# State-space stage of a two-block network: squares in eight tiles, two G and two V tables under the input product, lag zero on TensorE, states a quarter ahead

## The chip, the cores and the metric

The kernel runs on one core of one Trainium2 chip. The metric is the device time of the launch in microseconds. A measurement is the median of several runs of the same program.

## The reference

The reference computes two blocks one after the other on a sequence of 512 tokens of width 1024, in float32. The change touches only the first layer of the first block, the state-space mixer:

```python
u = (rms_norm(x) @ w_in).reshape(seq, 64 groups, 16)
a = exp(lam * step)                      # complex, 64 states per group
bu = einsum('gnk,lgk->lgn', b * f, u)    # complex
x_l = a * x_(l-1) + bu_l                 # scan over the 512 tokens
y = real(einsum('gkn,lgn->lgk', c, x)) + d_skip * u
z = gelu(y);  val, gate = split(z @ w_glu);  x = x + val * sigmoid(gate)
```

Behind it come a feed-forward layer, a latent attention layer, a second feed-forward layer and the whole second block (three kinds of attention in two layers).

## The kernel before

The kernel is written in raw instructions: every engine has a program of its own in the order in which it is to run, and semaphores join them. Nothing is planned by a compiler, so an instruction that waits holds all that stands behind it on its engine.

Matrix products use split operands. A weight block of 128 output channels (1024 inputs) is loaded by SP into one of four `raw` slots (`load`), ScalarE writes its high half `wh` (L583, `split_high`), VectorE the low half `wl` (L1088, `split_low`), each with two slots, and `product` (L1819) runs 24 matmuls of 512 columns: high by high, high by low, low by high (L1828 to L1830). `ahead` splits the block two places ahead.

The input product (stage `w_in`, blocks 0 to 7) takes `xH` and `xL`, which ScalarE (L597) and VectorE (L1094) make tile by tile. In product 0 each of the eight input tiles is followed by a matmul of ones by its square (L1967); the squares go through two buffers, so ScalarE (L600) waits on TensorE (`sq_used`). `inverse_root` (L607) turns their sum into the row `R`. Between the tiles VectorE computes the factors of the recurrence (`denominator`, `input_gain`, `powers`, `gained`, all through L1128), then `input_sums` and `output_sums`. Each finished block is multiplied by `R` into `T` (L1274) and written by SP to DRAM (L434), from where `read_u` (L418) reads it back with channels and time rearranged, eight transfers per quarter into `U`. Quarter 1 lies over `T[0:2]`, so its read waits for all eight blocks.

The recurrence is done in chunks of eight steps, in four quarters of 16 groups. For a quarter q:

- `make_g(q)` (VectorE, L1213 on, five instructions of 128x1024) makes the table G, of which there is one; `from_g` (TensorE, L1867) transposes it into `WM` through ScalarE copies (L641, `copy_w`), `lags` (L1878) multiplies it by `C2` (ScalarE, L650) into the lag weights, and `lag0` (VectorE, L1283 on) adds the skip term to them and writes them as the last row of `MS`. SP copies that row seven times, shifted (`mat_shift`, L429).
- `make_v(q)` (POOL, L484 to L488, five instructions of 128x1024) makes the table V. There is one, so for q above 0 it waits for `y_ready` of the quarter before.
- `states(q)` (TensorE, L1893) makes the chunks' inputs; VectorE rotates them by the phases `Er`, `Ei` (six instructions), scans (L1326, two) and rotates back into `state` (six).
- `outputs(q)`: the Toeplitz part (L1906: `MS` by `U`), then the state part (L1914: V by `state`), which sets `y_ready`. ScalarE applies gelu (L691), `turn_z` (L1924) transposes, ScalarE and VectorE split the result into `zH` (L677) and `zL` (L1303).

POOL makes the phase tables before V: five rounds of doubling, then the last third alone (L526 to L528); VectorE makes the other part in `last_phases` (L1232), after block 6. TensorE's order is: products 0 to 6, `from_g(0)`, `lags(0)`, product 7, and then for each quarter `states(q)`, `from_g(q+1)`, `turn_z(q-1)`, `lags(q+1)`, `outputs(q)`; in the last quarter half of the first two glu blocks (L1938 to L1940) goes in front of `outputs`. VectorE's order in a quarter is: rotation, `zL` of the quarter before, scans, state, `make_g(q+2)`, `lag0(q+1)`; `make_g(1)` and `lag0(0)` stand between product 7 and the first rotation. SP's order behind the input product is, for each quarter, the seven shifts of `MS`, the wait for `y_ready`, and the eight reads of the quarter two ahead.

## Time and profile before

| what | value |
|---|---|
| median of 3 runs | 1985.24 us (1982.36 to 1986.06) |
| profiled execution | 1985.31 us, span 1983.5 us |
| granted TensorE clock over the span | 0.977 |
| TensorE busy | 1860.6 us (94%), 8948 matmuls |
| VectorE busy | 1068.1 us (54%) |
| ScalarE busy | 833.3 us (42%) |
| GpSimd (POOL) busy | 131.8 us (7%) |
| HBM traffic | 143.83 MB read, 4.19 MB written |

In the profile PE is TensorE's matmuls and PEld its weight loads, DVE is VectorE, ACT ScalarE, POOL GpSimd, SP the engine that issues most transfers; the letter q behind an engine is its sequencer. A group names line, engine, operation, output and inputs. "Idle before" is the time for which the engine stood still just before, and the name behind the arrow is what ended it. PEclk is the granted clock as a share of 2.4 GHz. Times are from the span's start.

### The profile page before, as it was taken

What the parts mean: (1) busy time and instruction counts of PE and PEld (TensorE: products, weight loads), DVE (VectorE), ACT (ScalarE), POOL (GpSimd) and SP (SyncE); (2) the same over time, 40 slices, a digit from 0 to 9 for tenths busy, and PEclk for the clock granted to TensorE, in tenths of its full rate; (3) what the DMA queues carried; (4) which work ended last, traced back from release to release, by engine and by line L of the source; (5) the groups of instructions that cost most, each with busy time, mean ns of one, the idle gap of its engine ahead of it and who ended that gap; (6) DMA issues with size and microseconds to landing.
All of it is one profiled execution on the core that took longest, in us unless ns stands there. A gap on an engine that the chain in (4) does not pass through costs nothing.

```text
span 1983.5 us, 24248 instructions
## 1 busy us (share of the span) xinstructions
PE 1860.6 (94%) x8948; PEld 1429.4 (72%) x8948; DVE 1068.1 (54%) x1640; ACT 833.3 (42%) x1393; POOL 131.8 (7%) x164
## 2 busy tenths in 40 slices
PE   6787999999999889989999999999999989999997
PEld 4676878888888656657888888778666667866665
DVE  7695454444433657746444434464555375456537
ACT  4231344444223556744444422232566532266653
POOL 7543000000000000000000000001000000100000
PEclk9888999999999999999999999999999999999998
DMA  4320322222333110112222233312111022311111
GB/s 171 98 51 32 104 88 95 95 96 100 92 97 102 45 33 26 60 41 92 99 95 95 95 93 93 101 68 92 54 54 54 33 85 75 96 54 43 54 34 63
DMA packets 56827, 151.18 MB, mean 76 GB/s; under 512 B 15744, under 2 KB 20640, under 8 KB 56736
## 3 DMA queue, kind: packets, MB, share of 16 engines
q1 hardware_dynamic: 55232, 148.31, 22.7%
q0 software_dynamic: 1504, 1.64, 0.3%
q8 instruction: 59, 0.97, 0.2%
q14 instruction: 32, 0.26, 0.0%
HBM read 143.83 MB, written 4.19 MB: 75 GB/s over the span
## 4 chain that ended last, share of the span: by engine, by line
PE 84%; DVE 10%; ACT 4%; issue 2%; DMA 0%; POOL 0%; DVEq 0%; SPq 0%; ACTq 0%
PE bank L1828 17%; PE bank L1829 17%; PE bank L1830 17%; PE bank L2312 3%; PE bank L2314 3%; PE bank L2313 3%; PE bank L2289 2%; PE bank L2274 1%; PE bank L2275 1%; PE bank L2273 1%; PE bank L2033 1%; DVE wl L1088 1%; DVE G L1128 1%; PE bank L2061 1%; ACT wh L583 1%
## 5 line engine op out<-in xcount | busy, mean ns | idle before, releaser
L1088 DVE TENSOR_TENSOR wl<-raw,wh 128x1024 fp32r<-128x1024 f32 (+3 forms) x280 | 324.5, 1159 | 545.8 <-ACT wh L583 543.2
L583 ACT ACTIVATE wh<-raw 128x1024 fp32r<-128x1024 f32 (+3 forms) x280 | 279.0, 997 | 617.6 <-PE bank L1830 520.6
L1828 PE MATMUL bank<-xH,wh 128*128 128x512 f32 x896 | 358.6, 400 | 11.4 <-DVE wl L1088 9.5
L1829 PE MATMUL bank<-xL,wh 128*128 128x512 f32 x896 | 350.7, 391 | 0.0
L1830 PE MATMUL bank<-xH,wl 128*128 128x512 f32 x896 | 350.5, 391 | 0.0
L1828 PEld LDWEIGHTS bank<-xH,wh 128*128 128x128 f32 x896 | 169.6, 189 | 53.6 <-issue 15.7
L1829 PEld LDWEIGHTS bank<-xL,wh 128*128 128x128 f32 x896 | 169.5, 189 | 38.9 <-issue 4.1
L1830 PEld LDWEIGHTS bank<-xH,wl 128*128 128x128 f32 x896 | 169.3, 189 | 35.8
L1828 PE MATMUL bank<-hidH,wh 128*128 128x512 f32 x352 | 137.3, 390 | 0.0
L1830 PE MATMUL bank<-hidH,wl 128*128 128x512 f32 x352 | 136.9, 389 | 0.0
L1829 PE MATMUL bank<-hidL,wh 128*128 128x512 f32 x352 | 136.9, 389 | 0.0
L2312 PE MATMUL bank<-xH,wh 128*128 128x512 f32 x256 | 109.8, 429 | 10.7 <-ACT qk L961 7.1
L2314 PE MATMUL bank<-xH,wl 128*128 128x512 f32 x256 | 101.5, 396 | 0.0
L2313 PE MATMUL bank<-xL,wh 128*128 128x512 f32 x256 | 100.9, 394 | 0.0
L1728 DVE TENSOR_REDUCE least<-bank 128x1 f32<-128x128 f32 (+3 forms) x96 | 42.5, 485 | 73.8 <-PE bank L2296 73.8
L952 ACT ACTIVATE Pm<-bank,least 128x128 f32<-128x128 f32 (+3 forms) x96 | 49.9, 525 | 68.5 <-DVE least L1728 68.4
L1829 PEld LDWEIGHTS bank<-hidL,wh 128*128 128x128 f32 x352 | 66.1, 188 | 14.0 <-issue 0.2
L1828 PEld LDWEIGHTS bank<-hidH,wh 128*128 128x128 f32 x352 | 66.1, 188 | 13.9 <-issue 0.2
L1830 PEld LDWEIGHTS bank<-hidH,wl 128*128 128x128 f32 x352 | 66.1, 188 | 13.8
L2312 PEld LDWEIGHTS bank<-xH,wh 128*128 128x128 f32 x256 | 48.7, 190 | 22.0 <-issue 15.7
L720 ACT ACTIVATE hidH<-T 128x512 f32 (+1 forms) x44 | 27.8, 632 | 78.6 <-DVEq L1374 78.6
L552 POOL DMA_DIRECT2D rope_cos<-con_dram x2 | 1.1, 556 | 884.7 <-PE bank L2218 884.7
(424 smaller groups left out, 3311.7 us busy)
## 6 DMA issues: line engine op xcount, KB each, us to landing
raw<-w_gu_dram SPq DMA_DIRECT2D x88, 512.0 KB, 3.4
raw<-w_p_dram SPq DMA_DIRECT2D x64, 512.0 KB, 3.4
raw<-w_dn_dram SPq DMA_DIRECT2D x32, 448.0 KB, 3.3
raw<-w_glu_dram SPq DMA_DIRECT2D x16, 512.0 KB, 3.6
raw<-w_dn_dram SPq DMA_DIRECT2D x16, 512.0 KB, 3.5
raw<-w_out_dram SPq DMA_DIRECT2D x16, 512.0 KB, 3.5
raw<-w_in_dram SPq DMA_DIRECT2D x8, 512.0 KB, 7.8
raw<-w_o_dram SPq DMA_DIRECT2D x8, 512.0 KB, 3.4
```

The costliest lines, as they stand in the source:

```text
L583: nc.scalar.activation(wh[:, (st.base + u) % 2, 0:kts * P], raw[:, (st.base + u) % 4, 0:kts * P], ACT.Copy).then_inc(w_high, 1)
L720: nc.scalar.activation(hidH[:, bass.ds(2 * i + u // 2, 1), :].rearrange("p o n -> p (o n)"), T[:, 3, :], ACT.Copy).then_inc(sem("hid_high" ...
L952: nc.scalar.activation(Pm[side][:, POFF[j]:POFF[j] + w], banks[side][:, 0:w], ACT.Exp, scale=-1.0, bias=least[:, j, side:side + 1], accum_ ...
L1088: nc.vector.tensor_tensor(wl[:, s, 0:kts * P], raw[:, (st.base + u) % 4, 0:kts * P], wh[:, s, 0:kts * P].bitcast(F32), ALU.subtract).then_ ...
L1728: nc.vector.tensor_reduce(least[:, j, side:side + 1], banks[side][:, 0:(j + 1) * P], AX, ALU.min)\
L1828: nc.tensor.matmul(bank, wh[:, s, w], hi[:, k, :], start=first and kt == 0, stop=False)
L1829: nc.tensor.matmul(bank, wh[:, s, w], lo[:, k, :], start=False, stop=False)
L1830: ins = nc.tensor.matmul(bank, wl[:, s, w], hi[:, k, :], start=False, stop=last and kt == kts - 1)
L2289: nc.tensor.matmul(banks[side][:, 0:w], qk[half_of(side), m, j * P:w], qk[half_of(side), 8 + m, 0:w], start=True, stop=False)
L2312: nc.tensor.matmul(bank, wh[:, s, w], xH[:, kt, :], start=kt == 0, stop=False)
L2313: nc.tensor.matmul(bank, wh[:, s, w], xL[:, kt, :], start=False, stop=False)
L2314: ins = nc.tensor.matmul(bank, wl[:, s, w], xH[:, kt, :], start=False, stop=kt == KD - 1)
```

## The change

The state-space stage is put in another order, with more buffers:

- the eight squares get a tile each (four in `T`, two in `sq`, `acc`, `sd`), and their matmuls stand in one block behind product 1; the ones come from the constants, which SP loads earlier, and the loads of blocks 1 to 3 change places with `Bz` and `Cz`;
- the input blocks use other banks (`in_bank`), so that banks 1, 2 and 0 come free for `states(0)` and `lags(1)`;
- `make_g(0)` is cut in two parts, between evictions; its transposes and lag weights stand behind product 4; `make_g(1)` stands behind the eviction of block 4, `states(0)` and the first half of `from_g(1)` before product 7;
- V has buffers of its own for quarters 1 and 3; `make_v(0)` goes in front of POOL's last phases, `make_v(1)` behind the eviction of block 7;
- lag zero: POOL writes a table `skip_rows` once, TensorE adds it with one matmul per quarter into the lag bank, ScalarE copies the sum to `MS` (`copy_lags`), and VectorE's `lag0` goes;
- `states(q+1)` stands in front of `outputs(q)`.

The diff, shortened (a line of dots stands for removed lines that the kernel above shows; many lines are moved to the left):

```diff
@@ -243,0 +244 @@
+    zH_mem = Region(nc, s5.base + s5.at + 8 * KB, 8 * KB)
@@ -244,0 +246 @@
+    zL_mem = Region(nc, s5.base + s5.at + 4 * KB, 4 * KB)
@@ -257,0 +260,3 @@
+    VM1 = [zL_mem.tensor("VM1r", [P, QP, P]), zH_mem.tensor("VM1i", [P, QP, P])]
+    VM3 = [T[:, 2:4, :].rearrange("p a (b c) -> p (a b) c", c=P), core.tensor("VM3i", [P, QP, P])]
+    skip_rows = zH_mem.tensor("skip_rows", [GK, NG, GK])
@@ -352,0 +358,9 @@
+    def vm(q, ri):
+        return VM1[ri] if q == 1 else VM3[ri] if q == 3 else VM[:, ri, :, :]
+    def x_square(k):
+        return T[:, k, :] if k < 4 else (sq[:, 0, :], sq[:, 1, :], acc[:, :], sd[:, :])[k - 4]
+    def in_bank(n):
+        return banks[(0, 1, 2, 3, 1, 2, 0, 3)[n]][:, :]
@@ -408 +421,0 @@
-    sp.dma_start(Bz[:, 0:2, :, :].rearrange("p a b c -> p (a b c)"), ssm_b).then_inc(sem("b_loaded"), 16)
@@ -410 +422,0 @@
-    sp.dma_start(Cz[:, 0:2, :, :].rearrange("p a b c -> p (a b c)"), ssm_c).then_inc(sem("c_loaded"), 16)
@@ -411,0 +424,4 @@
+    load(stages["w_in"], 0, 2)
+    sp.dma_start(Bz[:, 0:2, :, :].rearrange("p a b c -> p (a b c)"), ssm_b).then_inc(sem("b_loaded"), 16)
+    sp.dma_start(Cz[:, 0:2, :, :].rearrange("p a b c -> p (a b c)"), ssm_c).then_inc(sem("c_loaded"), 16)
+    load(stages["w_in"], 0, 3)
@@ -415 +431 @@
-    for u in range(2, 8):
+    for u in range(4, 8):
@@ -481,3 +497 @@
-        if q:
-            pool.wait_ge(sem("y_ready"), q)
-        v0, v1 = (VM[:, ri, :, :].rearrange("p q (l k) -> p q l k", l=CH) for ri in range(2))
+        v0, v1 = (vm(q, ri).rearrange("p q (l k) -> p q l k", l=CH) for ri in range(2))
@@ -512 +526 @@
-    nc.gpsimd.memset(C2[:, :, :, :, :, :], 0.0).then_inc(sem("zeroed"), 1)
+    nc.gpsimd.memset(C2[:, :, :, :, :, :], 0.0).then_inc(sem("pool_tables"), 1)
@@ -519,0 +534,6 @@
+        if n == 4:
+            pool.wait_ge(sem("con_loaded"), 16)
+            pool.wait_ge(sem("mix_loaded"), 48)
+            nc.gpsimd.tensor_tensor(skip_rows[:, :, :], skip[0:GK, :].unsqueeze(2).to_broadcast([GK, NG, GK]),
+                                    const("lag0")[0:GK, :].unsqueeze(1).to_broadcast([GK, NG, GK]), ALU.mult)\
+              .then_inc(sem("pool_tables"), 1)
@@ -522,0 +543,4 @@
+    pool.wait_ge(sem("powers_ready"), 1)
+    pool.wait_ge(sem("sq_used"), KD)
+    pool.wait_ge(sd_ready, 1)
+    make_v(0)
@@ -525,0 +550 @@
+    pool.wait_ge(sem("v_ready"), 1)
@@ -530,3 +554,0 @@
-    pool.wait_ge(sem("powers_ready"), 1)
-    pool.wait_ge(sem("sq_used"), KD)
-    make_v(0)
@@ -537,3 +559,9 @@
-    pool.sem_inc(sem("zeroed"), 1)
-    for q in range(1, NQ):
-        make_v(q)
+    pool.sem_inc(sem("pool_tables"), 1)
+    make_v(1)
+    pool.wait_ge(sem("v_ready"), 2)
+    pool.wait_ge(sem("y_ready"), 1)
+    make_v(2)
+    pool.wait_ge(sem("v_ready"), 3)
+    pool.wait_ge(sem("u_written2"), 32)
+    pool.wait_ge(sem("u_written3"), 32)
+    make_v(3)
@@ -595,2 +623 @@
-        if n:
-            act.wait_ge(x_ready, 8 * (n - 1) + k + 1)
+        act.wait_ge(x_ready, 8 * (n - 1) + k + 1)
@@ -598,2 +625 @@
-        if isinstance(k, int) and k >= 2 or n:
-            act.wait_ge(sem("sq_used"), 8 * n + k - 1)
+        act.wait_ge(sem("sq_used"), 8 * n + k - 1)
@@ -622,2 +648,2 @@
-        prepare(0, k, "mix0", xH)
-        if k == 0:
+        nc.scalar.activation(xH[:, k, :], xT[:, k, :], ACT.Identity, scale=column("mix0", k)).then_inc(high_ready, 1)
+        if k == 1:
@@ -628 +654 @@
-        if k == 1:
+        if k == 2:
@@ -630,2 +656 @@
-        if k == 3:
-            split_high(stages["w_in"], 0, 1)
+    split_high(stages["w_in"], 0, 1)
@@ -633,2 +658,3 @@
-    act.wait_ge(sem("sq_used"), KD)
-    inverse_root(R[:, :], banks[7][:, :], 1.0 / D, sd_ready)
+    def x_squares(ks):
+        for k in ks:
+            nc.scalar.activation(x_square(k), xT[:, k, :], ACT.Square).then_inc(sq_ready, 1)
@@ -636,2 +662,2 @@
-    def copy_w(q):
-        for h in range(4):
+    def copy_w(q, hs):
+        for h in hs:
@@ -643,0 +670,8 @@
+    def copy_lags(q):
+        act.wait_ge(sem("lag_made"), q + 1)
+        if q:
+            act.wait_ge(sem("toeplitz_used"), q)
+        nc.scalar.activation(MS[:, CH - 1, :, :], lag_bank(q)[:, 0:QG * GK].rearrange("p (g k) -> p g k", g=QG), ACT.Copy)\
+          .then_inc(sem("lag_ready"), 1)
@@ -662 +696,2 @@
-    for n in range(KD):
+    def next_block(n):
@@ -664,8 +699,24 @@
-        if n == 3:
...
-            copy_w(0)
+    x_squares(range(4))
+    next_block(0)
+    x_squares(range(4, KD))
+    next_block(1)
+    act.wait_ge(sem("sq_used"), KD)
+    inverse_root(R[:, :], banks[7][:, :], 1.0 / D, sd_ready)
+    act.wait_ge(sem("powers_ready"), 1)
+    act.wait_ge(sd_ready, 1)
+    nc.scalar.activation(banks[7][:, :].rearrange("p (r l q) -> p r l q", r=2, l=CH), pf[:, 0:2, :, :], ACT.Copy)\
+      .then_inc(sem("pf_copied"), 1)
+    next_block(2)
+    act.wait_ge(sem("pool_tables"), 1)
+    lag_weights(0)
+    next_block(3)
+    next_block(4)
+    copy_w(0, (0, 1))
+    copy_w(0, (2, 3))
+    next_block(5)
+    lag_weights(1)
+    next_block(6)
+    copy_w(1, (0, 1))
+    next_block(7)
+    copy_w(1, (2, 3))
@@ -679 +730,2 @@
-    act.wait_ge(sem("zeroed"), 2)
+    act.wait_ge(sem("pool_tables"), 3)
+    copy_lags(0)
@@ -681,0 +734 @@
+    decay_rows(1)
@@ -683,4 +736,2 @@
-        if q + 1 < NQ:
-            lag_weights(q + 1)
-            copy_w(q + 1)
-            decay_rows(q + 1)
+        if q and q + 1 < NQ:
+            copy_w(q + 1, (0, 1))
@@ -688,0 +740,7 @@
+        if q and q + 1 < NQ:
+            copy_w(q + 1, (2, 3))
+            decay_rows(q + 1)
+        if q + 2 < NQ:
+            lag_weights(q + 2)
+        if q + 1 < NQ:
+            copy_lags(q + 1)
@@ -1212 +1270 @@
-    def make_g(q):
+    def make_g(q, parts=(0, 1)):
@@ -1221,10 +1279,13 @@
-        tt(t, ps, br, ALU.mult)
...
-        dve.sem_inc(sem("g_ready"), 1)
+        if 0 in parts:
+            tt(t, ps, br, ALU.mult)
+            if q:
+                dve.wait_ge(sem("lag_made"), q)
+                dve.wait_ge(sem("wt_ready"), 4 * q)
+            else:
+                dve.wait_ge(sem("pf_copied"), 1)
+            tt(G[:, 0], pi, b_sum, ALU.mult)
+            tt(G[:, 0], t, G[:, 0], ALU.subtract)
+        if 1 in parts:
+            tt(G[:, 1], pr, b_gap, ALU.mult)
+            tt(G[:, 1], G[:, 1], t, ALU.add)
+            dve.sem_inc(sem("g_ready"), 1)
@@ -1242,2 +1302,0 @@
-    step(nc.vector.memset(T[:, 2, 0:P], 1.0))
-    dve.sem_inc(sem("tiny_ready"), 1)
@@ -1244,0 +1304,18 @@
+    st = stages["w_in"]
+    def x_low(k):
+        dve.wait_ge(high_ready, k + 1)
+        nc.vector.scalar_tensor_tensor(xL[:, k, :], xT[:, k, :], column("mix0", k), xH[:, k, :].bitcast(F32),
+                                       ALU.mult, ALU.subtract).then_inc(h_ready, 1)
+    def next_block(n):
+        ahead(st, n // 4, n % 4, n >= 4)
+    def take_input(j):
+        dve.wait_ge(w_used, st.base + j + 3)
+        if j >= 4:
+            dve.wait_ge(sem(f"u_written{j % 4}"), 16)
+        step(nc.vector.tensor_tensor(T[:, j % 4, :], in_bank(j), R[:, :], ALU.mult))
+        dve.sem_inc(evicted, 1)
+        dve.sem_inc(sem("u_ready"), 1)
@@ -1246,4 +1323 @@
-        prepare(0, k, "mix0", xH, xL)
-        if k == 1:
-            split_low(stages["w_in"], 0, 0)
-            denominator()
+        x_low(k)
@@ -1251,10 +1325,10 @@
-            input_gain()
...
-            gained()
+            split_low(st, 0, 0)
+    split_low(st, 0, 1)
+    denominator()
+    input_gain()
+    powers(1)
+    powers(2)
+    next_block(0)
+    powers(4)
+    gained()
+    next_block(1)
@@ -1262,0 +1337,8 @@
+    dve.wait_ge(sd_ready, 1)
+    take_input(0)
+    take_input(1)
+    next_block(2)
+    make_g(0, (0,))
+    take_input(2)
+    next_block(3)
+    make_g(0, (1,))
@@ -1267,31 +1349,10 @@
-    dve.wait_ge(sd_ready, 1)
...
-        dve.sem_inc(sem("lag_ready"), 1)
+    take_input(3)
+    next_block(4)
+    take_input(4)
+    make_g(1)
+    take_input(5)
+    next_block(5)
+    last_phases()
+    take_input(6)
+    next_block(6)
+    take_input(7)
@@ -1305,2 +1365,0 @@
-    make_g(1)
-    lag0(0)
@@ -1334,0 +1394,2 @@
+        if q == 0:
+            next_block(KD - 1)
@@ -1337,2 +1397,0 @@
-        if q + 1 < NQ:
-            lag0(q + 1)
@@ -1858 +1917 @@
-    def from_g(q):
+    def from_g(q, hs):
@@ -1861 +1920 @@
-        for h in range(4):
+        for h in hs:
@@ -1873,0 +1933,2 @@
+        elif q == 0:
+            pe.wait_ge(sem("pool_tables"), 2)
@@ -1874,0 +1936,4 @@
+        if q == 1:
+            pe.wait_ge(evicted, KD + 3)
+        nc.tensor.matmul(lag_bank(q)[:, 0:QG * GK], const("ident")[0:GK, :],
+                         skip_rows[:, q * QG:(q + 1) * QG, :].rearrange("p g k -> p (g k)"), start=True, stop=False, skip_group_check=True)
@@ -1879 +1944,2 @@
-                                       C2[:, q % 2, ri, pair, :, :].rearrange("p g k -> p (g k)"), start=ri == 0, stop=ri == 1)
+                                       C2[:, q % 2, ri, pair, :, :].rearrange("p g k -> p (g k)"), start=False, stop=ri == 1,
+                                       skip_group_check=True)
@@ -1889 +1955 @@
-            pe.wait_ge(evicted, tiles["w_glu"] + 4)
+            pe.wait_ge(evicted, KD + 2)
@@ -1901,2 +1967,3 @@
-        if q:
-            pe.wait_ge(h_ready, KD + 2 * q)
+        pe.wait_ge(h_ready, KD + 2 * q)
+        if q == 0:
+            pe.wait_ge(evicted, KD + 4)
@@ -1914 +1981 @@
-                    ins = nc.tensor.matmul(y(pair, h), state[halves(h), ri, pair, :], VM[halves(h), ri, pair, :],
+                    ins = nc.tensor.matmul(y(pair, h), state[halves(h), ri, pair, :], vm(q, ri)[halves(h), pair, :],
@@ -1946,2 +2013,8 @@
-        i, u = n // 4, n % 4
-        pe.wait_ge(evicted, n + 1)
+        if n:
+            pe.wait_ge(evicted, (2, 3, 4, 6, 7, 7, 8)[n - 1])
+            if n == 7:
+                states(0)
+                from_g(1, (0, 1))
+            product(st, n // 4, n % 4, xH, xL, in_bank(n))
+        else:
+            product(st, 0, 0, xH, xL, in_bank(0), tile_ready=1)
@@ -1950,2 +2023,6 @@
-        if n == KD - 1:
-            from_g(0)
+            for k in range(KD):
+                pe.wait_ge(sq_ready, k + 1)
+                nc.tensor.matmul(banks[7][:, :], const("ones"), x_square(k), start=k == 0, stop=k == KD - 1)\
+                  .then_inc(sem("sq_used"), 1)
+        if n == 4:
+            from_g(0, (0, 1))
@@ -1953,16 +2030 @@
-        if n:
...
-              .then_inc(sem("sq_used"), 1)
+            from_g(0, (2, 3))
@@ -1971,2 +2033,5 @@
-    for q in range(NQ):
-        states(q)
+    from_g(1, (2, 3))
+    lags(1)
+    states(1)
+    outputs(0)
+    for q in range(1, NQ):
@@ -1974,3 +2039,2 @@
-            from_g(q + 1)
-        if q:
-            turn_z(q - 1)
+            from_g(q + 1, (0, 1))
+        turn_z(q - 1)
@@ -1977,0 +2042 @@
+            from_g(q + 1, (2, 3))
@@ -1978,0 +2044 @@
+            states(q + 1)
@@ -1980,0 +2047 @@
+            pe.wait_ge(sem("lag_ready"), NQ)
```

## Rows read from the trace of the kernel before

**Rows 1.** Windows of stages: length, busy PE, PEld, DVE, ACT, POOL; clock, DMA, GB/s.
```profile
0.00:36.16 36.16, 18.48 (x41) 9.79 (x42) 26.53 (x75) 16.07 (x24) 24.50 (x67) 0.92 0.53 194
36.16:88.70 52.54, 47.41 (x217) 38.60 (x215) 32.55 (x28) 12.11 (x18) 37.94 (x30) 0.92 0.33 105
88.70:188.20 99.50, 72.27 (x1002) 66.85 (x1001) 81.62 (x87) 20.87 (x42) 39.18 (x18) 0.85 0.18 49
...
198.20:1983.50 1785.30, 1714.21 (x7604) 1307.88 (x7604) 924.76 (x1448) 779.83 (x1303) 30.18 (x50) 0.99 0.23 75
```

**Rows 2.** Chain of waits, first four products: start, us, what.
```profile
12.67 0.43 PE bank L1962
...
13.52 1.71 PE bank L1967 x2
...
53.56 1.07 ACT wh L583
```

**Rows 3.** Timeline, squares and sums: start, us, engine, what [idle].
```profile
29.27 1.02 PE L1967 MATMUL bank<-sq,T 128*128 128x512 f32 x2
...
35.41 2.15 DVE L1128 TENSOR_TENSOR Cz<-Cz 128x512 f32<-128x512 f32 x2
```

**Rows 4.** Timeline: G table of quarter 0, the stall, the stage's end.
```profile
56.74 2.93 DVE L1128 TENSOR_TENSOR tv<-pf,Bz 128x1024 f32<-128x1024 f32 x1
...
59.71 1.22 DVE L1128 TENSOR_TENSOR G<-bank,Bz 128x1024 f32<-128x1024 f32 x1
...
69.10 0.76 PE L1828 MATMUL bank<-xH,wh 128*128 128x512 f32 x1 [4.75 <-DVE wl L1088]
...
88.91 0.69 DVE L1274 TENSOR_TENSOR T<-bank,R 128x512 f32<-128x512 f32 x1 [2.63 <-PE bank L1830]
```

**Rows 5.** Timeline of quarter 0: SP reads U, DVE to the state.
```profile
91.90 3.76 SPq L421 DMA_DIRECT2D U<-u_dram  x8
...
98.64 0.69 DVE L1128 TENSOR_TENSOR rotr<-bank,Er 128x512 f32<-128x512 f32 x1 [0.22 <-DVE MS L1296]
...
103.11 1.23 DVE L1326 TENSOR_TENSOR_SCAN rotr<-rho,rotr 128x512 f32<-128x512 f32 x1
...
109.25 0.68 DVE L1128 TENSOR_TENSOR state<-rott,rotu 128x504 f32<-128x504 f32 x1
110.07 1.23 DVE L1128 TENSOR_TENSOR tv<-pf,Bz 128x1024 f32<-128x1024 f32 x1
```

**Rows 6.** Groups by line, 90 to 198 us: busy, mean ns | idle.
```profile
L1906 PE MATMUL bank<-MS,U 128*64 128x128 f32 x128 | 12.2, 370 | 3.1 <-DVE zL L1303 1.8 <-DMA MS<-MS 1.2
L1878 PE MATMUL bank<-C,G 128*128 128x32 f32 x96 | 11.7, 282 | 0.0
...
L1893 PE MATMUL bank<-U,WM 128*64 128x64 f32 x256 | 8.5, 224 | 1.0 <-DVEq L1275 1.0
L1924 PE MATMUL bank<-cons,zs 64*64 64x64 f32 x256 | 8.3, 220 | 0.0
L1867 PE MATMUL bank<-cons,G 128*128 128x128 f32 x48 | 8.3, 331 | 7.3 <-DVEq L1230 6.8 <-ACT WM L641 0.5
...
L1326 DVE TENSOR_TENSOR_SCAN rotr<-rho,rotr 128x512 f32<-128x512 f32 x4 | 7.1, 1768 | 0.0
...
L1128 DVE TENSOR_TENSOR rotr<-rotr,rott 128x512 f32<-128x512 f32 x4 | 5.4, 1358 | 0.1
...
L1128 DVE TENSOR_TENSOR tv<-skip,cons 128x256 f32<-128x256 f32 x4 | 4.9, 1222 | 0.6
```

**Rows 7.** Timeline: the last two state outputs [idle before].
```profile
158.26 6.28 PE L1914 MATMUL bank<-VM,state 64*64 64x128 f32 x64 [4.42 <-DVEq L1334]
...
182.85 5.38 PE L1914 MATMUL bank<-VM,state 64*64 64x128 f32 x64 [4.24 <-DVEq L1334]
```

**Rows 8.** Waits, 89 to 190 us: total, times, longest.
```profile
POOL tp L484 <- PE bank L1914: 47.2, 3, 21.9
```

**Rows 9.** Window of a short stretch: granted clock.
```profile
158.00:162.00 4.00, 3.74 (x36) 3.77 (x38) 0.90 (x3) 0.00 (x0) 0.00 (x0) 0.50 0.07 16
```

66 lines of the change are left out of this document (2 added, 64 removed).

## The prediction

> **What bounds the kernel now.** I read the windows of five stages first, then the chain of waits through the first 200 us, then the timelines and the groups by line of that stretch. The span is 1983.5 us; 1785 us of it lie behind 198.2 us, where TensorE is busy for 1714 us, and no line of the change works there, so it keeps its time [rows 1]. What can move is the first 198 us, and in it three things are to be seen.
>
> First, the input product. Until 36.16 us TensorE is busy for only 18.48 us [rows 1]: product 0 is interleaved with eight squares products, whose tiles ScalarE may write only two ahead, and VectorE does its small tables between the low halves. Product 3 ends at 53.5, where ScalarE's next split is let go [rows 2]. Then the G table of quarter 0 (L1128, from 56.74) stands on VectorE in front of the low half of block 5, and TensorE waits 4.75 us for it at 69.10 [rows 4]. The last product ends at 88.7. Call that point M.
>
> Second, from M to the first rotation VectorE takes 9.9 us (88.7 to 98.64), because the G table of quarter 1, two lag-zero sums and the state product all stand there [rows 4, 5]. Third, the four quarters follow each other at VectorE's pace: rotation, scans and state sums take 11.3 us (98.64 to 109.93), a G table 6.3 (five instructions of 1.23 with their gaps), two lag-zero sums more (4.9 us in four for the first of them), two zL sums 1.4 (two of the 0.69 size) [rows 5, 6]. In the last two quarters the chain also holds TensorE's state output, 6.28 and 5.38 us, and the next quarter's state product, 2.1 (8.5 in four), behind it [rows 6, 7]. The end of the last one, 188.23, is M + 99.5.
>
> **The change, part by part.**
>
> *Squares and products 0 to 3.* Product 0 starts where it did, at 11.9. The low-clock matmul is 0.43 and the full-clock one 0.226 (1714.21 by 7604) [rows 2, 1]. Of product 0's 24 matmuls I put 12 at 0.43 (the clock rose near 17 before too) and 12 at 0.226: 5.1 + 2.8, end 19.8. Product 1 is 24 x 0.226 = 5.4: 25.2. Eight squares products follow, none waiting for a buffer since each has a tile. One costs 0.86 at full clock (the pair of rows of 1.02 overlaps its follower by 0.16) and 1.71 at the low one [rows 2, 3]; I take 0.86 because TensorE has then run 13 us without a gap: 6.9, end 32.1. The other end costs 6.8 more. Products 2 and 3 end at 43.0 instead of 53.5. The blocks' loads now wait for nothing new: the constants go out in front of block 2, and at the 194 GB/s of this stretch all of it moves in the same 36 us [rows 1]; I cost the reordered issues on SP at nothing, and at most 2 us if block 1 came late.
>
> *The G table of quarter 0.* VectorE loses the squares' waits, but its small sums are the same and end at 37.6 as before (35.41 + 2.15) [rows 3]; R is ready by 34, so these sums are what is late next. Behind them: two evictions (0.69 + 0.24 each) 39.5, the split of block 4 1.8 (41.3), the first half of the table 2.93 + 1.22 + 2.1 (the last an estimate midway between 1.23 and 2.93) with gaps (47.6), an eviction, a split (50.3) and the second half 1.23 + 1.7: ready at 53.3. I take the slow 2.93, not the 1.23 of the same instruction alone, since POOL's phase tables run here [rows 4, 5]. Product 4 ends at 48.5, so TensorE waits 4.8 us: the old stall is moved, not removed. The transposes (8.3 in three, 2.8 with gaps; 2.4 here), the lag product (11.7 in three, 3.9) and one more matmul per quarter for lag zero (16 rows by 256 columns; between nothing and the 0.86 of a square with twice the columns, 0.5) follow [rows 3, 6]: 60.1. Behind the wait of 4.75 the first matmul took 0.76 [rows 4]; half a product at the low clock is lost again, 12 x (0.43 - 0.226) = 2.4.
>
> *Products 5, 6, 7.* 3 x 5.4 from 60.1 + 2.4, and in front of the last one the states of quarter 0, 2.1 [rows 6], and half of quarter 1's transposes, 1.1, both moved from behind M. Sum 81.9; VectorE's second G table fits under product 5 and costs nothing there unless the table of quarter 0 slips. I take M = 81.5, since the low clock may end within the lags. Against 88.7: **7.2 us**. Ends: 3 us more gain without stall, nothing gained if the squares run at the low clock.
>
> *Quarter 0 behind M.* The eviction (0.8) and then the rotation: the state product is there already. POOL must have done its last phases: they start 14.4 us later, behind V of quarter 0, and end near 78 to 80, within 1 us of need. I cost them at nothing and keep 2 us for the range. Rotation to state 11.3; but POOL now makes V of quarter 1 beside it, where it waited before (47.2 us of waits for y) [rows 8]. The price: a sum of two SBUF tiles took 1.358 on average against 0.69 for one fed by a bank, the scan 1.768 against 1.23 [rows 5, 6]; over three tables these two groups alone make 4.9 us, 1.6 per table. If every such instruction beside a table of some 12.4 us (39.18 in three [rows 1]) were 2.4 times as long, as 2.93 to 1.23 is, it would be 6. I take 3.5. State of quarter 0: M + 15.6. The Trainium skill (GPSIMD Engine Reference, Key points) says that POOL shares its SBUF interfaces with VectorE, and contends with instructions of two SBUF inputs. By it quarter 0 must pay; were it as clean as before, the sum would be 3.5 us better. The bank-fed 1.22 beside POOL agrees with the rule [rows 4].
>
> *Quarters 1 to 3.* VectorE: split of block 7 1.3, G table 6.3, rotation 4.5 and half a contention 1.7: M + 29.4; zL 1.4; scans and state sums 6.8 + 1.8: 39.4. G table 6.3 + 1.7, rotation 4.5 + 1.0, zL 1.4, scans and sums 6.8: 61.1. The lag-zero sums are gone (4.9 us in four, and the four MS sums) [rows 6]; their copies go to ScalarE, busy for 20.87 of the 99.5 us [rows 1]. Rotation of quarter 3 needs no output of quarter 2 any more (its states were made a quarter ahead), but its scans stand behind zL of quarter 2: state output 5.0 from 61.3, then gelu 0.6, turn 2.1 (8.3 in four [rows 6]) and copy and subtraction 0.7 each of the last half, about 4.0, so 70.3; scans and sums 6.8: 77.1; last state output 5.38 [rows 7]: M + 82.6. Against 99.5: **16.9 us**. TensorE's own order per quarter (transposes 2.8, turn 2.1, lags 4.4, states 2.1, Toeplitz 3.1, state output 5) is 19.5 and lies beside VectorE's 21 [rows 6]. SP is the third queue: for quarter 2 the seven shifts (5.2) and eight reads of U (3.76 [rows 5]) end near M + 30, and states are wanted at 33; 3 us of cover, and 6 us or so over three quarters if it is gone.
>
> **Sum.** 7.2 + 16.9 = 24.1; with the first piece of glu unchanged, the profiled execution's 1985.3 us (span 1983.5) would be 1961. It stands 0.1 us above the median of the runs shown, 1985.24.
>
> **The rivals.**
>
> *More than that* (0.17). The contention is the 1.6 of the two groups (three times 1.9 less), no stall stands before the G table (4.8 and 2.4), and the state output, less often behind an idle engine, takes some 3.7 us (an estimate: 6.28 has 4 us at half the level) rather than 5: 5.7 + 7.2 + 3 on top, 1945. For it: that output's two values [rows 7]. Against: POOL's tables are as many as before.
>
> *One stretch gains, the other doesn't* (0.19). Either M stays, because squares at the low clock (6.8) eat its gain, giving 1968; or the loop is held by SP's reads behind the shifts and by contention of 6 per table (7.5 + 6), giving 1974. The change would then not do what it says: states a quarter ahead, which wait for U. Against: 3 us of cover.
>
> *Slower: TensorE at 1.2 GHz* (0.05). The rows show it: TensorE idle for 4.42 us up to 158.26, granted 0.50 from 158 to 162, and a state output of 6.28 there [rows 7, 9]. New waits stand before the G table and before each state product; were each product cold, it would cost 24 x (0.43 - 0.226) = 4.9 us more, eight of them 39, and four state outputs 2.6 each, 10: 1961 + 49 = 2010. It decides against the kernel from six cold products on (29 us). Against: in rows where products follow each other the level is full. The Trainium skill (TensorE: Matmul & The Clock Gate, section HAM oscillation — how this bites in real kernels) says that bursts divided by waits may each start at the low clock; by that rule I would have 2010, and the trace agrees only behind idle stretches of 4 us and more.
>
> *No net change* (0.03): 1985, both offsets at once.
>
> **How the numbers follow.** The forecast holds 0.56: 1961, itself 1955 to 1968. The range leaves out the slower rival, no change and the far ends: 1944 to 1975. A measurement of this kernel can tell some 0.2% (4 us) from no change. Faster: 0.56 + 0.17 + 0.19 less 0.02 for far ends = 0.90; same 0.04; slower 0.06.
>
> **What would show it.** M near 81.5 and the squares in one block from 25 to 32; if that block takes 13 us, the clock step is wrong. TensorE idle for 3 to 6 us before the transposes of quarter 0; none, and the G table was quicker than I took it. The first rotation 0.8 us behind M; if later, POOL's last phases or states. The last state output ending at M + 83. The idle of the quarters' state product put down to U's DMA would show SP's queue as the bound. If the stage behind changes by more than 2 us, a cover that I did not see was gone.

## The result, and the profile after

| | before | after |
|---|---|---|
| median, beside each other | 1982.22 us (1979.64 to 1986.06) | 1975.08 us (1973.35 to 1977.48) |
| profiled execution, its span | 1985.3, 1983.5 | 1974.36, 1972.5 |

The ratio of the two medians is 0.996, with a 95% interval of 0.9948 to 0.9972. The forecast was 1961 with a range of 1944 to 1975. The direction was right. The gain was 7 us where 24 were forecast, and the result lies just outside the range. The two profiled executions are 11.0 us apart by their spans: the one of before is 3.1 us above its median and the one of after 0.7 us below. So of the 17 us that are missing from the gain, the traces below can account for 13; the other 4 are these two offsets, chiefly that the forecast started from 1985.3, near the upper end of what the kernel before takes.

The windows of the changed kernel are cut at the end of the input product (79.0, the point M), at the end of the last state output (177) and at the end of the span. Columns as in [rows 1].

```profile
0.00:79.00 79.00, 65.27 (x331) 51.73 (x332) 67.30 (x105) 30.07 (x48) 64.88 (x95) 0.96 0.45 156
79.00:177.00 98.00, 71.44 (x936) 65.78 (x934) 83.92 (x76) 20.07 (x40) 47.22 (x21) 0.81 0.19 52
177.00:1972.00 1795.00, 1723.12 (x7692) 1314.96 (x7692) 927.59 (x1451) 784.35 (x1309) 30.19 (x50) 0.99 0.24 75
```

M came 9.7 us earlier than the 88.7 of before. But the stretch from M to the last state output shrank only from 99.5 to 98.0, although VectorE has 76 instructions there for 87. Its busy time did not fall with them (81.62 in [rows 1], 83.92 now): what is left takes longer. The rest of the kernel kept its time: 1795.3 us behind 188.2 before, 1795.5 behind 177 now.

The timeline shows where. First TensorE: the squares, then the wait for the G table of quarter 0, the last matmul of the input product, and a wait behind it (columns: start, us, engine and line, what, and in brackets the idle time before it and who ended it).

```profile
25.27 3.59 PE L2025 MATMUL bank<-T,cons 128*128 128x512 f32 x8
...
31.27 1.02 PE L2025 MATMUL bank<-sd,cons 128*128 128x512 f32 x2
...
50.12 1.09 PE L1926 MATMUL bank<-cons,G 128*128 128x128 f32 x8 [1.50 <-DVEq L1291]
...
78.76 0.39 PE L1889 MATMUL bank<-xH,wl 128*128 128x512 f32 x1
78.99 1.03 PE L1926 MATMUL bank<-cons,G 128*128 128x128 f32 x8
88.22 1.22 PE L1938 MATMUL bank<-skip_rows,cons 16*128 16x256 f32 x2 [8.19 <-ACT MS L675]
```

The squares stand in one block of seven us at the full level (granted 1.00 from 25 to 32), and TensorE waits 1.50 us for the table instead of 4.75 [rows 4]. The last row shows a new wait: behind M TensorE stands for 8.19 us until ScalarE has copied the lag-zero block, and ScalarE waits for POOL, which zeroes MS only behind its V table and its phases.

The same stretch on POOL:

```profile
62.50 3.02 POOL L498 TENSOR_TENSOR tp<-Cz,pw 128x1024 f32<-128x1024 f32 x1 [0.28 <-POOL sm L513]
...
74.01 3.26 POOL L502 TENSOR_TENSOR VM<-VM,tp 128x1024 f32<-128x1024 f32 x1
77.35 2.78 POOL L551 TENSOR_TENSOR Er<-Er,sm 128x1024 f32<-128x1024 f32 x1
...
83.05 2.32 POOL L553 TENSOR_TENSOR Er<-Er,tp 128x1024 f32<-128x1024 f32 x1
...
85.89 1.80 POOL L558 MEMSET MS<- 128x2048 f32 x1
```

And on VectorE, from its own last phases to the state of quarter 0:

```profile
68.63 3.41 DVE L1186 TENSOR_TENSOR Ei<-Er,sm 128x1024 f32<-128x1024 f32 x1
...
81.13 0.68 DVE L1318 TENSOR_TENSOR T<-bank,R 128x512 f32<-128x512 f32 x1
85.45 0.69 DVE L1186 TENSOR_TENSOR rotr<-bank,Er 128x512 f32<-128x512 f32 x1 [3.64 <-POOLq L554]
...
90.48 2.92 DVE L1385 TENSOR_TENSOR_SCAN rotr<-rho,rotr 128x512 f32<-128x512 f32 x1
...
103.95 0.68 DVE L1186 TENSOR_TENSOR state<-rott,rotu 128x504 f32<-128x504 f32 x1
```

The first rotation waits for POOL's last phases (3.64 us), and from there to the state it takes 19.2 us (to 104.63), where it took 11.3 before [rows 5]: the V table of quarter 1 now runs beside it, and the scan that took 1.23 takes 2.92. M does not set when that rotation starts. In the seven runs, of this kernel and of those below, in which V of quarter 0 stands in front of POOL's last phases, the last matmul of the input product ended anywhere from 75.3 to 80.9 us, and the rotation began at 85.3 to 85.7 in all of them. So POOL's chain is the bound there, and an earlier M is cover. Quarter 1 meets the tables of quarters 2 and 3, and quarter 2 meets none:

```profile
121.67 3.21 DVE L1385 TENSOR_TENSOR_SCAN roti<-rho,roti 128x512 f32<-128x512 f32 x1
124.92 2.33 DVE L1186 TENSOR_TENSOR rott<-rotr,Er 128x512 f32<-128x512 f32 x1
...
129.70 2.70 DVE L1186 TENSOR_TENSOR state<-rott,rotu 128x504 f32<-128x504 f32 x1
...
151.75 1.23 DVE L1385 TENSOR_TENSOR_SCAN roti<-rho,roti 128x512 f32<-128x512 f32 x1
153.01 0.69 DVE L1186 TENSOR_TENSOR rott<-rotr,Er 128x512 f32<-128x512 f32 x1
```

### The profile page after: what moved, and what is told of

It is laid out like the page before. It is cut to its first block, busy times and chain, and to the rows that moved or that the text cites. A ratio compares the mean times of both kernels' runs of the same rounds, so it can differ in the third digit from the quotient of the medians.

```text
span 1972.5 us, 24263 instructions
## 1 busy us (share of the span) xinstructions
PE 1859.8 (94%) x8956; PEld 1432.5 (73%) x8956; DVE 1078.8 (55%) x1631; ACT 834.5 (42%) x1397; POOL 142.3 (7%) x165
## 4 chain that ended last, share of the span: by engine, by line
PE 82%; DVE 8%; ACT 4%; POOL 4%; issue 2%; DMA 0%; SPq 0%; DVEq 0%; ACTq 0%; POOLq 0%
PE bank L1887 17%; PE bank L1888 17%; PE bank L1889 17%; PE bank L2379 3%; PE bank L2381 3%; PE bank L2380 3%; PE bank L2356 2%; PE bank L2342 1%; PE bank L2341 1%; PE bank L2340 1%; PE bank L2100 1%; DVE wl L1146 1%; PE bank L2465 1%; PE bank L2128 1%; PE bank L2468 1%
## 5 line engine op out<-in xcount | busy, mean ns | idle before, releaser
L2379 PE MATMUL bank<-xH,wh 128*128 128x512 f32 x256 | 109.7, 428 | 10.7 <-ACT qk L1019 7.1
L2379 PEld LDWEIGHTS bank<-xH,wh 128*128 128x128 f32 x256 | 48.9, 191 | 21.7 <-issue 15.4
```

The lines of the kernel that those rows point to most:

```text
L2379: nc.tensor.matmul(bank, wh[:, s, w], xH[:, kt, :], start=kt == 0, stop=False)
```

## The experiments

Two theories. **Turns:** an instruction of VectorE and one of POOL that both read SBUF take turns, so a V table costs VectorE by how many such instructions it meets; that, and POOL's own chain in front of the first rotation, ate the gain. **Rival:** the order of work on TensorE and the reads of U on SP hold the quarters, and the slower VectorE costs nothing. Each run is compared with runs of the kernel before beside it; "ratio" is to these, with its 95% interval. Where a run is set against the changed kernel, medians are compared: with 1975.08 up to the run that repeats the changed kernel, and with its 1973.4 from there on.

### The disputed cost alone

A kernel of its own, which computes nothing of the reference: VectorE runs short series of one instruction, first alone, then with a series of POOL products started beside each.

```diff
+for part, body in enumerate((lambda: two(6), lambda: banked(8), lambda: single(8), lambda: two(6, 1024), lambda: two(10))):
+    dve.sem_inc(go, 1)
+    dve.wait_ge(ready, part + 1)
+    body()
...
+PN = [(6, 1024), (6, 1024), (6, 1024), (6, 1024), (16, 256)]
```

> Leaves out the whole network; it times VectorE instructions alone and beside POOL products of 1024 or 256 elements a partition, and copies x to the output. Theory P (the two engines take turns at SBUF, one instruction at a time): a VectorE product of two SBUF tiles of 512 elements takes 0.69 us alone and as long as the POOL instruction beside it, 2.0 to 2.8 us, when POOL's has 1024 elements, but under 1.2 us when POOL's has 256; 1024 elements take 2 to 3 us too; with one input from a bank it stays at 0.69. Rival R (the bandwidth is shared): the product of two SBUF tiles takes about twice its time, 1.4 us for 512 and 2.5 us for 1024, whatever POOL's length is. A tensor_scalar with one SBUF input: no view, 0.3 to 2.5 us.

Its timeline. Rows of several instructions (x6) give the time of all of them:

```profile
11.38 2.87 DVE L57 TENSOR_TENSOR dout<-da,db 128x512 f32<-128x512 f32 x4
...
17.18 1.81 DVE L65 TENSOR_SCALAR dout<-da 128x512 f32<-128x512 f32 x4
19.14 14.42 DVE L57 TENSOR_TENSOR dout<-da,db 128x512 f32<-128x512 f32 x6
19.30 16.46 POOL L89 TENSOR_TENSOR pout<-pa,pb 128x1024 f32<-128x1024 f32 x6 [7.78 <-DVEq L70]
35.90 5.77 DVE L61 TENSOR_TENSOR dout<-bank,db 128x512 f32<-128x512 f32 x8 [2.35 <-POOLq L87]
...
50.59 15.76 DVE L65 TENSOR_SCALAR dout<-da 128x512 f32<-128x512 f32 x8 [8.91 <-POOLq L87]
...
66.60 17.62 DVE L57 TENSOR_TENSOR dout<-da,db 128x1024 f32<-128x1024 f32 x6 [0.26 <-POOLq L87]
...
86.56 10.86 DVE L57 TENSOR_TENSOR dout<-da,db 128x512 f32<-128x512 f32 x10 [2.34 <-POOLq L87]
86.64 16.17 POOL L89 TENSOR_TENSOR pout<-pa,pb 128x256 f32<-128x256 f32 x16 [0.23 <-DVEq L70]
102.90 9.59 POOL L92 TENSOR_TENSOR pout<-pa,pb 128x1024 f32<-128x1024 f32 x4
```

A product of two SBUF tiles takes 0.72 us alone (2.87 by 4) and 2.40 beside POOL's 1024-wide products (14.42 by 6), which alone take 2.40 each (9.59 us for four) and here 2.74 (16.46 by 6). Twice as wide, it takes 2.94, not twice 2.40, and beside POOL products of a quarter of the width it takes 1.09, while POOL ends about one product of its own for each of VectorE's (10.86 us at 1.01 each are 10.7, against 10). So the price is not a share of the bytes: each instruction of VectorE, its own time included, takes about as long as one instruction of POOL. Fed by a bank the product stays at 0.72; a `tensor_scalar`, with one SBUF input, goes from 0.45 (1.81 by 4) to 1.97 (15.76 by 8). The Trainium skill (SBUF — State Buffer, section Who interferes with whom) gives as the reason an exclusive lock held for a whole instruction, by VectorE instructions of two SBUF inputs and by copies and scalar forms in a mode that takes both ports. The rows agree on both kinds; they do not show the lock itself, and its length not quite: one instruction of each engine in turn would make 0.72 + 2.40 = 3.12 us, and 2.40 to 2.74 were measured, so the two overlap in part.

### The V tables left out

POOL makes the V table of quarter 0 alone, and the outputs of quarters 1 to 3 use it too.

```diff
-        return VM1[ri] if q == 1 else VM3[ri] if q == 3 else VM[:, ri, :, :]
+        return VM[:, ri, :, :]
...
-            make_v(1)
...
-            make_v(3)
+            pool.wait_ge(sem("v_ready"), 1)
+            pool.sem_inc(sem("v_ready"), 3)
```

> The changed kernel without POOL's V tables of quarters 1 to 3: outputs use the V of quarter 0. Theory P (behind the input product the quarters are held by what POOL's tables do to VectorE's sums): rotation to state falls from 19.2 us in quarter 0 and 24.7 in quarter 1 to 11.3 and 12.6, and the kernel gains 17 to 22 us over the changed one, 1955 us. Rival Q (the quarters are held by TensorE's order and by SP's reads of U): it gains under 4 us.

1953.35 us (1951.99 to 1956.36), ratio to before 0.9848 [0.9824, 0.9871]: 21.7 us under the changed kernel. From rotation to state quarter 0 takes 11.3 us again:

```profile
85.70 0.69 DVE L1180 TENSOR_TENSOR rotr<-bank,Er 128x512 f32<-128x512 f32 x1 [5.64 <-POOLq L554]
...
90.16 1.22 DVE L1379 TENSOR_TENSOR_SCAN rotr<-rho,rotr 128x512 f32<-128x512 f32 x1
...
96.30 0.68 DVE L1180 TENSOR_TENSOR state<-rott,rotu 128x504 f32<-128x504 f32 x1
```

The three tables cost 21.7 us, 7.2 each on average. In the traces the last state output ends 22.0 us earlier (154.95 for 176.98). With the order of TensorE and SP untouched the end moved by all of it, so these two do not hold the quarters: the rival falls.

### POOL's last phases first

```diff
             pool.sem_inc(sem("phases_ready"), 1)
-            pool.wait_ge(sem("powers_ready"), 1)
-            pool.wait_ge(sem("sq_used"), KD)
-            pool.wait_ge(sd_ready, 1)
-            make_v(0)
             wr, wi = (v(f"u1{c}").unsqueeze(2).to_broadcast([P, NPAIR, NCH // 2]) for c in "ri")
...
             pool.sem_inc(sem("phases_ready"), 1)
+            pool.wait_ge(sem("powers_ready"), 1)
+            pool.wait_ge(sem("sq_used"), KD)
+            pool.wait_ge(sd_ready, 1)
+            make_v(0)
+            pool.wait_ge(sem("v_ready"), 1)
```

> The changed kernel with POOL's last phases in front of V of quarter 0 again, as in the kernel before. Theory P: the first rotation starts at 82 us instead of 85.45, and 2 to 3.5 us of it reach the end, 1972 us. Rival Q: the start moves, and the state output of quarter 0 does not (it waits for the Toeplitz part, which ends at 102.8), so under 1 us reaches the end.

1973.43 us (1972.6 to 1974.8), 0.9944 [0.9922, 0.9966]: not to be told from the changed kernel, as the rival had it. The rotation began 1.7 us earlier, at 83.77. That it was not more lies in this execution and not in the edit: its input product ended only at 82.2, behind a wait of 3.00 us for the G table and a granted clock of 0.67 from 50 to 60, and with the same order on POOL the rotation begins at 79.3 in a later run. The wait for POOL is gone, but its V table of quarter 1 starts at 87.5 all the same, behind that of quarter 0, and now meets the last sum of the rotation as well as the scans (2.53, then 2.92 us), so the state comes at 104.2 instead of 104.6. Nor could a still earlier rotation have helped much, since ScalarE wrote the decay rows that the scan reads only at 87.66 to 88.78:

```profile
83.77 0.69 DVE L1186 TENSOR_TENSOR rotr<-bank,Er 128x512 f32<-128x512 f32 x1 [0.32 <-DVE T L1318]
...
87.66 1.12 ACT L691 ACTIVATE rho<-sm 128x504 f32<-128x504 f32 x2
```

### The V tables behind the state products

```diff
             pool.sem_inc(sem("pool_tables"), 1)
+            pool.wait_ge(sem("s_ready"), 1)
             make_v(1)
...
             pool.wait_ge(sem("y_ready"), 1)
+            pool.wait_ge(sem("s_ready"), 2)
             make_v(2)
...
             pool.wait_ge(sem("u_written3"), 32)
+            pool.wait_ge(sem("s_ready"), 3)
             make_v(3)
```

> The changed kernel; V of quarter q starts when the state of quarter q-1 is made, so that it stands beside the split, the G table and the rotation and not beside the state sums. Theory P: a slowed state sum costs 1.7 us for each POOL instruction beside it, and the G and rotation stretch 3 to 5 us per table, so the three tables cost 12 us instead of 21: 6 to 9 us gained over the changed kernel, 1968 us. Rival Q: no change. If a table costs the same wherever it stands, no change either, with the long sums now in the G table.

1963.81 us (1963.02 to 1965.28), 0.99 [0.9877, 0.9922]: 11 us under the changed kernel, 2 more than I gave it at most. The tables are all there; only what they meet is different. On VectorE behind the state of quarter 0:

```profile
96.77 3.09 DVE L1149 TENSOR_TENSOR wl<-raw,wh 128x1024 fp32r<-128x1024 f32 x1
99.78 3.04 DVE L1189 TENSOR_TENSOR tv<-pf,Bz 128x1024 f32<-128x1024 f32 x1
102.86 1.22 DVE L1189 TENSOR_TENSOR G<-bank,Bz 128x1024 f32<-128x1024 f32 x1
104.11 2.00 DVE L1189 TENSOR_TENSOR G<-tv,G 128x1024 f32<-128x1024 f32 x1
106.15 1.22 DVE L1189 TENSOR_TENSOR G<-bank,Bz 128x1024 f32<-128x1024 f32 x1
```

A table beside a G table and a rotation meets rows fed by a bank in between (1.22, unchanged). Beside two scans and six state sums, all of SBUF tiles, it has a partner for each instruction. Whether it was the second V buffer that gave this placing away is asked further down.

### The V buffers undone

The changed kernel itself was run once more beside the next three.

> The changed kernel itself once more, on the chip of the three runs beside it. Both theories: 1975 (1973 to 1977), 0.4 to 0.5% under the kernel before. It is there so that the three others can be set against it within one job.

1973.4 us (1973.24 to 1975.6), 0.9952 [0.9938, 0.9966]. Then one V table again, released by the output of the quarter before:

```diff
-        return VM1[ri] if q == 1 else VM3[ri] if q == 3 else VM[:, ri, :, :]
+        return VM[:, ri, :, :]
...
-            make_v(1)
...
-            make_v(3)
+            for q in range(1, NQ):
+                pool.wait_ge(sem("y_ready"), q)
+                make_v(q)
```

> The change's two V tables put back to one: POOL makes V of quarter 1, 2 and 3 only when the output of the quarter before it has been read, as it did before. Theory of turns (what the change lost is the V tables running ahead, beside the scans and the state sums, whose every instruction reads SBUF alone): the sums of quarter 0 run free (11.3 us from rotation to state, not 19.2), the tables fall on the G table and the rotation, most of whose instructions read a bank; some 10 us gained over the changed kernel, 1965 (1962 to 1968). The V table of quarter 3 then ends last, near 160, and the last state output waits for it by a few us. Rival (TensorE's own order of work and the reads of U on SP hold the quarters): V comes later and nothing else changes, so 1975 to 1985.

1971.02 us (1968.26 to 1972.38), 0.9935 [0.9911, 0.9959]: 2.4 us under the changed kernel, not 10, with intervals that overlap. A miss, and a useful one. The sums of quarter 0 ran free, to 96.66, as expected. But the output that releases POOL came late. TensorE:

```profile
88.14 1.22 PE L1933 MATMUL bank<-skip_rows,cons 16*128 16x256 f32 x2 [9.55 <-ACT MS L670]
89.29 7.04 PE L1938 MATMUL bank<-C,G 128*128 128x32 f32 x32
96.25 3.74 PE L1954 MATMUL bank<-U,WM 128*64 128x64 f32 x64
99.72 2.61 PE L1968 MATMUL bank<-MS,U 128*64 128x128 f32 x32
102.26 3.71 PE L1976 MATMUL bank<-VM,state 64*64 64x128 f32 x64
```

The state was there at 96.7, the output ended at 106.0, because TensorE had stood 9.55 us for MS and then done lags, states and Toeplitz one after the other, the lags at the low level (granted 0.50 from 88 to 98; 7.04 us for what takes 3.76 in quarter 1). The first table therefore began at 106.07 and met the scans of quarter 1 (3.19) after all; the third met those of quarter 3 (3.25), and the last state output behind them, after 6.33 idle us, took 6.18 instead of 3.71. The rival has this much in it: TensorE's order is not the bound, but what POOL's zeroing holds back there decides when the tables start.

### The states put back behind the outputs

```diff
             lags(1)
-            states(1)
             outputs(0)
+            states(1)
...
                     lags(q + 1)
-                    states(q + 1)
...
                 outputs(q)
+                if q + 1 < NQ:
+                    states(q + 1)
```

> The states of quarters 1 to 3 put back behind the output of the quarter before; all else as changed. The timeline of the changed kernel gives: rotation of quarter 1 not later (the G table of quarter 2 ends at 113.5, after the states would), rotation of quarter 2 by 1 us, rotation of quarter 3 from 157.5 to some 164 (output of quarter 2 ends at 162.2, states 2.1), of which 2.9 us were idle time anyway: 3 to 6 us slower than the changed kernel, 1979 (1977 to 1981). Theory that contention alone sets the pace of all quarters: no change, 1975. If the states ahead carried most of the gain that I forecast for the quarters: 1985 or more.

1978.36 us (1976.66 to 1980.03), 0.9972 [0.9963, 0.9982]: 5.0 us above the changed kernel. By the ratios it is 4.0, with intervals that just overlap; its fastest execution, 1976.66, is slower than the slowest of the changed kernel beside it, 1975.6. This part of the change works, and is worth what the timeline says: nothing in quarter 1, 2.2 us at the rotation of quarter 2, and most at quarter 3, whose rotation no longer waits for the output of quarter 2 (166.21 here for 157.46).

### Both repairs, then POOL's zeroing

The first version has POOL's last phases in front of its V table of quarter 0 and the other tables behind the state products.

> V tables released by the state product of their quarter, and POOL's last phases before its V table of quarter 0. Alone the first gained 11 us over the changed kernel (1963.8) and the second 1.7 us at the first rotation, of which nothing was left at the end. Theory of turns: the second's gain was eaten by tables that start with the first rotation and run for a fixed time; with these gone it should come through, so 1960.5 (1959 to 1962.5). Rival (the end is held by something further back, such as the gelu and turn of quarter 2): as the first alone, 1963.8.

1963.68 us (1962.66 to 1964.09), 0.9901 [0.9878, 0.9923]: the same as with the tables behind the state products alone, and not the 1960.5 that I expected. The rotation did begin 6 us earlier, at 79.31; then VectorE stood again:

```profile
84.83 1.16 DVE L1189 TENSOR_TENSOR roti<-roti,rott 128x512 f32<-128x512 f32 x1
88.75 1.22 DVE L1388 TENSOR_TENSOR_SCAN rotr<-rho,rotr 128x512 f32<-128x512 f32 x1 [2.76 <-ACT rho L694]
```

ScalarE writes the decay rows rho behind its copy of the lag-zero block, and that copy waits until POOL has zeroed MS, which stood behind V of quarter 0 (85.86). So the zeroing was moved into that table, behind its third instruction, as soon as U is evicted. The cut is against the run just shown; `zero_buffers` holds the lines that are taken out here, and `make_v` calls it:

```diff
-            make_v(0)
+            make_v(0, zero_buffers)
             pool.wait_ge(sem("v_ready"), 1)
-            pool.wait_ge(sem("u_ready"), KD)
-            step(nc.gpsimd.memset(rho[:, :, :, 0:1], 0.0))
-            step(nc.gpsimd.memset(state[:, :, :, 0:1], 0.0))
-            step(nc.gpsimd.memset(MS[:, :, :, :], 0.0))
-            pool.sem_inc(sem("pool_tables"), 1)
```

> As the run with the last phases first and the V tables released by the state product, but POOL zeroes rho, the state's first column and MS between the third and the fourth instruction of its V table of quarter 0, as soon as U is evicted (near 79), not behind that table (85.5). In the run before, the first rotation began 6 us earlier (79.3) and VectorE then stood 2.76 us before the scan for ScalarE's decay rows, which stand behind the copy of the lag-zero block, and that behind these memsets. Theory (a chain POOL memset, ScalarE copy, decay rows took the place of the wait for the phases): the 2.76 us go, two V instructions fall beside the scans and cost 1 to 2, so 1962.5 (1961 to 1964). Rival (POOL's memsets don't matter, the end is held by the gelu and turn of quarter 2): 1963.7, as the run before.

1961.36 us (1960.44 to 1961.66), 0.9869 [0.9853, 0.9886]. The 2.76 us are gone, one scan takes 3.26, and the state of quarter 0 is there at 94.7 instead of 95.6. The last version also releases V of quarter 1 by the first product of the G table of quarter 2:

```diff
-            pool.wait_ge(sem("s_ready"), 1)
+            pool.wait_ge(sem("tv_made"), 1)
             make_v(1)
...
                     tt(t, ps, br, ALU.mult)
+                    if q == 2:
+                        dve.sem_inc(sem("tv_made"), 1)
```

> The same, and POOL's V table of quarter 1 is released by the first product of the G table of quarter 2, 4 us later than by the state product. Theory of turns: the low half of block 7 (3.09) and that product (3.04) go back to 1.23 each, 3.7 us; the table's last two instructions then fall on the rotation, 1 us, and perhaps one scan, 1 us. 1 to 3 us gained: 1960.5 (1959 to 1962). Theory of a shared bandwidth, in which POOL's bytes cost the same wherever they fall: no difference between the two.

1959.29 us (1957.77 to 1961.8), 0.9858 [0.9842, 0.9874]. The intervals overlap, so 2 us between the two are likely rather than shown; in the trace the first product takes 1.22 again and the scan of quarter 1 2.06. Of what was gained earlier, some is lost at the end. The last state output of this kernel and of the one with the tables behind the state products alone, in this order:

```profile
157.48 0.52 PE L1990 MATMUL bank<-T,state 64*64 64x128 f32 x4 [3.65 <-DVEq L1402]
157.72 0.70 PE L1990 MATMUL bank<-VM3i,state 64*64 64x128 f32 x4
...
161.35 0.41 PE L1990 MATMUL bank<-T,state 64*64 64x128 f32 x4
```

```profile
162.02 0.44 PE L1984 MATMUL bank<-T,state 64*64 64x128 f32 x4 [2.98 <-DVEq L1396]
162.26 0.41 PE L1984 MATMUL bank<-VM3i,state 64*64 64x128 f32 x4
```

After 2.98 idle us the matmuls run at the full level (granted 1.00 from 162 to 165.7), after 3.65 seven of these rows take 0.70 instead of 0.41 (granted 0.53 from 157.5 to 161). But the length of the idle stretch does not settle it alone. The output of quarter 0 in the changed kernel, and that of quarter 1 with one V table released by the outputs:

```profile
104.84 5.38 PE L1981 MATMUL bank<-VM,state 64*64 64x128 f32 x64 [2.09 <-DVEq L1393]
```

```profile
123.34 3.71 PE L1976 MATMUL bank<-VM,state 64*64 64x128 f32 x64 [3.61 <-DVEq L1388]
```

The first took 5.38 us behind only 2.09 idle ones (granted 0.68), the second 3.71 behind 3.61 (granted 1.00). In the first TensorE had been at the low level (granted 0.50 from 88 to 101), rose to the full one near 102, kept it through the idle stretch and fell back inside the output itself (0.50 from 105.5 to 108.5). In the second it had been granted 1.00 from 104 to 114 and 0.70 from there to 119.7. What decides between them stays open.

### Lag zero back on VectorE

```diff
+                if q == 0:
+                    lag0(0)
...
+                if q + 1 < NQ:
+                    lag0(q + 1)
...
-            copy_lags(0)
...
-                if q + 1 < NQ:
-                    copy_lags(q + 1)
```

`lag0` is that of the kernel before, and the matmul with the skip's rows is gone.

> The changed kernel with lag zero back on VectorE: the product with the skip and the sum onto the bank, two instructions per quarter, and no copy of it on ScalarE and no matmul with the skip's rows. Where the V tables run (quarters 0 and 1) VectorE is bound all the same, so all four pairs lie on the path: 4 x (1.23 + 0.45), some 6.5 us, less what the idle 2.9 us before the zL sums of quarter 2 takes up: 4 to 7 us slower than the changed kernel, 1978.5 (1977 to 1981). Rival (the part was off the path, ScalarE's copies and the matmul cost as much elsewhere): 1973.4, no change.

1975.73 us (1973.13 to 1976.11), 0.9937 [0.992, 0.9953]; the changed kernel has 0.9952 [0.9938, 0.9966], so no difference is shown, and the 4 to 7 us that I expected are not there. The pair costs little where no table runs, and much where one does:

```profile
90.63 2.12 DVE L1183 TENSOR_TENSOR tv<-skip,cons 128x256 f32<-128x256 f32 x1
...
145.26 0.43 DVE L1183 TENSOR_TENSOR tv<-skip,cons 128x256 f32<-128x256 f32 x1
```

The 1.22 that I had taken for this product [rows 6] was a mean over both kinds; the instruction itself is 0.43. An instruction more beside a table also takes a turn that another then does not lose: with both of them in it, the stretch from the rotation to the state of quarter 0 takes 19.6 us here for 19.2.

## Why the prediction was wrong

By its own steps, in the profiled execution:

| step | forecast | measured |
|---|---|---|
| M | 81.5 | 79.0 |
| M to the first rotation | 0.8 | 6.45 |
| rotation to state, quarter 0 | 14.8 | 19.2 |
| from there to the end of the rotation of quarter 1 | 13.8 | 14.1 |
| zL, scans and sums of quarter 1 | 10.0 | 19.6 |
| quarter 2, G table to state | 21.7 | 19.0 |
| quarter 3, to the last state | 16.0 | 15.8 |
| last state output | 5.4 | 3.9 |
| M to the end of the last state output | 82.6 | 98.0 |

- **The input product: right, but off the path.** The squares did run at the full level (6.9 forecast; 25.3 to 32), and M came 2.5 us before the forecast; that TensorE waited 1.50 for the G table and not 4.8 makes 3.3 of it by itself. My estimate of that table on VectorE was too slow: its first product took 1.65, not 2.93. But the 7.2 us (9.7 measured) were added to the sum as if all of it reached the end, and the first rotation waited for POOL. From before to after it came 13.2 us earlier, where the forecast had 16.3 (98.64 to 82.3).
- **The step that failed: "I take 3.5" for a V table beside VectorE's sums.** Measured by leaving them out, it is 7.2 per table, above even the 6 of my upper bound. The sum held 9.7 us for the three, and they cost 21.7: 12.0 us of the 15.4 by which that stretch is too long. That is the size; the mechanism was named rightly. I had taken the price from means over the stretch before [rows 6], where the tables waited for the outputs and fell only partly on scans and sums. I knew that they would now run beside quarter 0 and did not ask which instructions there have a partner: all eight behind the rotation. The bound was wrong too: 2.4 times the instruction's length holds for a wide one (2.93 to 1.23), but a 0.69 us sum also takes as long as one POOL instruction, 2.3 to 2.7 us, over three times its length. Nor does 6 follow from the numbers beside it: 12.4 us filled with instructions 2.4 times as long hold 7.2 us of loss. That this equals what was measured is chance.
- **The second one: POOL's last phases, costed at nothing with 2 us kept for the range.** They ended at 85.37, not at 78 to 80. The V table and the phases themselves took what they took before (14.8 and 8.0 us; 14.5 and 8.1). But POOL came to them 8.6 us later: its last round of doubling ended at 62.2, where it had ended at 53.6. Of this, 2.3 us are the table `skip_rows`, which the change adds to POOL and the forecast did not price, 0.4 a later start, and the rest slower small products all along the input product. Between 12.4 and 15.6, for one, five of them took 0.58 to 0.60 us beside VectorE's low halves, where the same five took 0.25 to 0.67 before. No run takes this part by itself. VectorE's own last phases, beside all this, took 3.41 us for a row of 1.22. The rotation waited 3.64 us, and began 3.15 behind the forecast's 82.3. Put right alone it gave nothing that a measurement shows: the tables took part of it, and behind it stood a third wait, for POOL's zeroing, which the text did not have at all.
- **The states ahead: right.** 5.0 us by undoing them; SP's queue, the rival's cause, does not appear among the waits of the state products behind M.
- **Lag zero: over-priced.** 4.9 us of products were counted; undoing the part shows no cost. The medians leave 0.7 to 2.3 us, and the ratios lean the other way.
- **The state output: the rival's 3.7 was right** for the two that lie on the chain (quarters 2 and 3, 3.71 each), and 5 too long there; off the chain, quarters 0 and 1 took 5.38 and 5.81. The slow rival's reading, that the trace of before has the low level only behind 4 us of idle time and more, was too narrow: an output there took 5.04 behind 3.62 (granted 0.73), and in the changed kernel it showed behind 2.09.
- **Together**, counted from the span's start: the forecast put the end of the last state output at 164.1, and it came at 177.0, 12.9 late (13.0 by the steps, which add up to 0.1 less than its sum). The first rotation makes 3.15 of it, the quarters with their tables 11.6 (4.4, 0.3 and 9.6 more, quarter 2 2.7 less), and the last quarter and output give 1.7 back.

The rival "one stretch gains, the other doesn't" came to 1974, and its 6 per table was the nearest price, but SP's reads, the other half of it, had no part. So its time came out near by luck. (It was worked out from three times 3.5 for the tables, while the sum holds 9.7 for them; with 9.7 it comes to 1975.) Of the 24 us forecast, the version that places tables, phases and zeroing differently gives 28 (0.9858 against its own runs of before, with a median of 1987.16; against the 1982.22 above it is 23). So about as much as was forecast was to be had, and it was lost in where POOL's work falls.
